# Retention heads scored in pairs, and three column sums moved from the index heads into the retention steps

## The chip, the cores and the metric

The kernel runs on one core of a Trainium2 chip. The metric is the device time of one execution in microseconds (us), lower is better. The core has a matrix engine (TensorE, PE in the profile; its weight loads are PEld), a vector engine (VectorE, DVE), an activation engine (ScalarE, ACT), GpSimd (POOL) and SyncE (SP), which issues most of the weight loads. Each engine works through its own instructions in the order written and waits on semaphores for the others. Matrix results land in PSUM banks of 128 x 512 floats.

## The reference, cut to what matters

Two transformer blocks on 256 tokens of width 1024, in float32. The second block has a modulation vector `mod = silu(c) @ w_ada + b_ada`, cut into six rows of 1024 (`sh1, sc1, g1, sh2, sc2, g2`), and three branches over one projection of the tokens. The part of concern:

```
mod = silu(c) @ w_ada + b_ada                     # sh1, sc1, g1, sh2, sc2, g2
# index scores (8 heads of 64): relu(q k^T), weighted, summed; top 64 keys of a query are kept
# retention (8 heads, keys of 64, values of 128):
scores = einsum('bnihd,bnjhd->bhnij', qc, kc) * intra_decay
o      = scores @ v + (carried state)             # here: one decayed 256 x 256 lower block matrix a head
y_ret  = (silu(g) * group_norm(o) * gain) @ w_ret_out
# sparse attention (8 heads of 64) over the kept keys
h  = h + g1 * ((ga*y_ret + gb*y_dsa) @ w_o)
u2 = rmsnorm(h)*(1 + sc2) + sh2 ;  h = h + g2 * experts(u2)
```

## The kernel before, in words

Every dense product is done in three passes of rounded float32 (high by high, high by low, low by high). Its weights pass as units of 128 x 1024: SP loads a unit, ACT writes its rounded high part (`split`, line 1158), DVE subtracts to get the low part (line 1911), PE multiplies it with the tokens (12 matrix instructions, lines 2924 to 2926, `three`). Between the small steps of the heads each engine's program has `fill(n)`, which puts in the next n units, so that PE has dense work while a head's softmax or decay is done by the others. The order on every engine is written out by hand.

Small products and transposes go into two "turn" banks that are used in turn. `plan_turns` lists their uses in order; `turn_bank` makes PE wait until the use two before has been copied out. Head scores go into the two banks of `sco`.

The modulation rows are accumulated over the weights of `w_ada`, leaving 128 partial rows in `mod`. They have to be added over the partitions and spread to all of them: PE multiplies 512 columns with a matrix of ones (`ada_sums`, line 3207) and ACT copies the bank back to `mod` (`ada_out`, `turned_copy`, line 1301). Of the twelve column blocks, nine are done earlier; the last three (9, 10, 11: the second halves of what scales and gates the expert part) are done in the stage looked at here.

The stages around the change, with their rows of the trace:

- Index heads (574 to 594.6 us). PE scores two heads at once from the upper and the lower half of the partitions (64 rows each) into the two score banks, then does `fill(IDX_FILL[g])`, then one `ada_sums`. ACT rectifies (line 1654), DVE adds to `mix` (lines 2458, 2460). After heads 1, 3 and 5 ACT has the copy of one column block. In the same stretch ACT and DVE prepare the retention gates (lines 1647, 2443, 2446).
- Retention (594.6 to 629.2 us), steps i = 0 to 8. PE: scores of head i into score bank i % 2 (lines 3546, 3547), one unit of dense work, then head i-1 is weighed (`weigh`, lines 3183 to 3185) from `probs_t`. PE scores head i once `decayed` says that head i-2 has been read. DVE, step i: decayed scores `probs_t = sco * decay` (line 2513), two of the sixteen rounds of the top-64 search (lines 2478, 2479), the low part of one unit, mean and variance of head i-1 (`ret_stats`, lines 2503, 2507), an evacuation of a dense block where one ends (line 1948), the gated product of head i-3 (`ret_out`, line 2494). POOL turns the variance into a scale (lines 984 to 1101). ACT, step i: the decay matrix of head i (`decay`, line 1681), the high part of one unit, in steps 0, 4 and 8 the tanh of a gate block (line 1247), then the scaled output of head i-2 (`ret_scale`, line 1668), which waits for POOL. `ret_scale` also frees the turn bank of that head.
- Start of the sparse attention (629.2 us on): PE scores sparse heads 0 and 1 (line 3561), does two units, transposes the gated retention rows (`turn_kept`, line 3143), ACT and DVE split them (lines 1283, 2045), and PE starts the product with `w_ret_out` (line 3027).

The column blocks are needed by DVE much later: line 2592 (`1 + sc2`), line 2878 and line 2900 (`g2`).

Of the kernel before, what the change touches and what calls it, by code (L numbers as in the profile page):

```python
# [11 lines left out]
ACT = mybir.ActivationFunctionType  # L12
AX = mybir.AxisListType

P = 128
D = 1024
S = 256
NT = S // P
DK = D // P
CHUNK = 64  # L20
HEADS = 8
W = 512
# [27 lines left out]
SC_W = P + S  # L50
# [20 lines left out]
RET_FILL = [1] * 9  # L71
# [91 lines left out]
def plan_turns():  # L163

    order = [(f"x1.{g}", "dve") for g in range(4)]
    order += [("bv", "act")]
    order += [(f"cl.{g}", "dve") for g in range(3)]
    order += [(f"qk{h}", "act") for h in range(2)]
    for h in range(HEADS + 2):
        if h + 2 < HEADS:
            order.append((f"qk{h + 2}", "act"))
        if 1 <= h <= HEADS:
            order.append((f"dap{h - 1}", "act"))
        if h == HEADS + 1:  # L180
            order.append(("oa.1", "dve"))
        if 2 <= h:
            order.append((f"dao{h - 2}", "dve"))
        if h == HEADS:
            order.append(("oa.0", "dve"))
    order += [("oa.2", "dve"), ("oa.3", "dve")]
    order += [("kr", "act")]
    for h in range(HEADS + 2):
        if 1 <= h <= HEADS:
            order.append((f"mp{h - 1}", "act"))  # L190
        if 2 <= h:
            order.append((f"mo{h - 2}", "dve"))
    order += [(f"mg.{g}", "dve") for g in range(4)]
    order += [(f"x2.{g}", "dve") for g in range(4)]
    order += [(f"ffn{e}", "dve") for e in range(N_FFN)]
    order += [("ad4", "act"), ("ad5", "act")]
    order += [(f"u.{g}", "dve") for g in range(4)]
    order += [("rt0", "act"), ("rt1", "act"), ("lt", "act"), ("rt2", "act"), ("lat", "act"), ("rt3", "act")]
    order += [("dt4", "act")]
    order += [(f"ad{n}", "act") for n in range(9, 12)]  # L200
    order += [(f"rto{h}", "act") for h in range(HEADS)]
    order += [("re.0", "dve"), ("re.1", "dve"), ("dsp0", "act"), ("re.2", "dve"), ("re.3", "dve")]
    for h in range(2, HEADS + 2):
        if h <= HEADS:
            order.append((f"dsp{h - 1}", "act"))
        if 2 <= h:
            order.append((f"dso{h - 2}", "dve"))
    order += [(f"mh.{g}", "dve") for g in range(4)]
    order += [(f"v.{g}", "dve") for g in range(4)]
    order += [("moe0", "dve"), ("moe0b", "dve")]  # L210
    order += [(f"moe{e}", "dve") for e in range(1, N_EXP)]
    order += [(f"moe{N_EXP - 1}b", "dve")]
    turns, count, names = {}, {"act": 0, "dve": 0}, []
    for number, (name, engine) in enumerate(order):
        count[engine] += 1
        turns[name] = (number, engine, count[engine])
        names.append(name)
    return turns, names
# [3 lines left out]
TURNS, TURN_NAMES = plan_turns()  # L222
# [127 lines left out]
def two_blocks(nc, ins, consts, one_hot_d, small_d, lambda_d, router_d, rel_rows, out):  # L350
    ctx = ExitStack()
    with ctx:
# [14 lines left out]
        def sem(name):  # L367
            return ctx.enter_context(nc.semaphore(name))
# [214 lines left out]
        ada_done = sem("ada_products_accumulated")  # L583
        shift_summed = sem("shift_and_scale_summed")
        shift_out = sem("shift_and_scale_copied")
        early_summed = sem("early_rows_summed")
        early_out = sem("early_rows_copied")
        gated_half = sem("retention_gates_begun")
# [544 lines left out]
        def _(act):  # L1133
# [259 lines left out]
            def ada_out(n0, n1):  # L1393

                for n in range(n0, n1):
                    turned_copy(f"ad{n}", [(mod[:, n * W:(n + 1) * W], bank_of(f"ad{n}"), 1.0)])
# [253 lines left out]
            for i in range(HEADS):  # L1650
                act.wait_ge(idx_scored, i + 1)
                if i >= 2:
                    act.wait_ge(idx_acc, i - 1)
                act.activation(probs[:, i % 2, 0, :], sco[:, i % 2, 0:SC_W], ACT.Relu).then_inc(relud, 1)
                if i % 2:
                    fill(IDX_FILL[i // 2])
                if i in (1, 3):
                    gate_rows(i // 2)
                if i in (1, 3, 5):
                    ada_out(9 + i // 2, 10 + i // 2)  # L1660

            def ret_scale(n):

# [10 lines left out]
            for i in range(HEADS + 2):  # L1674
                if i < HEADS:
                    if i < 2:
                        act.wait_ge(idx_acc, HEADS)
                    else:
                        act.wait_ge(decayed, i - 1)
                    g = float(np.log(np.float32(1.0 - 2.0 ** (-5.0 - i))))  # L1680
                    act.activation(probs[:, i % 2, 0, :], cst[:, C_DIST:C_DIST + SC_W], ACT.Exp, scale=g)\
                        .then_inc(decay, 1)
                if i <= HEADS:
                    fill(RET_FILL[i])
                if i >= 2:
                    ret_scale(i - 2)
            for i in range(HEADS + 2):
# [204 lines left out]
        def _(dve):  # L1892
# [695 lines left out]
            dve.nop().then_inc(evac["dve"], 1)  # L2588
            split_to(u_next + 4)
            dve.wait_ge(rows_in[0], 32)  # L2590
            dve.wait_ge(freed["act"], TURNS["ad9"][2])
            step.mark(dve.scalar_tensor_tensor(out=mod[:, 4 * D:5 * D], in0=mod[:, 4 * D:5 * D], scalar=1.0,
                                               in1=rows[:, 0, :], op0=ALU.add, op1=ALU.mult))
            rows_lo("mh", 1, 0.5)
# [267 lines left out]
            for p in range(1, N_EXP - 1):  # L2862
                u = gate_up_unit(p + 1) + AHEAD
                expert_lo(p)
                late = p + 2 < N_EXP and dense(p + 1) and not dense(p)
                for kt in (1, 3, 5):
                    if late and kt == 5:
                        split_around(u + 1 + kt // 2, lambda: expert_hidden(p + 1))
                    else:
                        split_to(u + 1 + kt // 2)  # L2870
                    side(p, kt)
                    if kt == 3 and closes_group(p):
                        slot_sums_lo(p)
                if p in (1, 2):
                    t = p - 1
                    dve.wait_ge(y_first_out, 2 * NT)
                    dve.wait_ge(freed["act"], TURNS["ad11"][2])
                    step(dve.tensor_tensor(y_first[t], y_first[t], mod[:, 5 * D:6 * D], ALU.mult))
                    step(dve.tensor_tensor(x[:, t, :], x[:, t, :], y_first[t], ALU.add))
                split_to(u + 4)  # L2880
                if p + 2 < N_EXP and not late:
                    expert_hidden(p + 1)
                side(p, "gate_up")
                split_to(u + 6)
                side(p, "down")
# [6 lines left out]
                                         op0=ALU.mult, op1=ALU.mult).then_inc(hid_ready, 1)  # L2892
                first_turn_lo(t)

            dve.wait_ge(freed["act"], TURNS["ad11"][2])
            halves = (slice(0, W), slice(W, D))
            for t in range(NT):
                for n, c in enumerate(halves):
# [19 lines left out]
        def _(pe):  # L2918
# [602 lines left out]
            for g in range(HEADS // 2):  # L3521
                if g:
                    pe.wait_ge(relud, 2 * g)
                halves = [slice(64 * a, 64 * a + 64) for a in range(2)]
                for a, r in enumerate(halves):
                    pe.matmul(sco[:, a, 0:P], idq_t[r, g, 0:P], idk_t[r, 0:P], start=True, stop=True)
                for a, r in enumerate(halves):
                    pe.matmul(sco[:, a, P:SC_W], idq_t[r, g, P:S], idk_t[r, 0:S], start=True, stop=True)\
                      .then_inc(idx_scored, 1)
                fill(IDX_FILL[g])  # L3530
                if g < 3:
                    ada_sums(9 + g, 10 + g)

            for i in range(HEADS + 1):
                if i == 0:
                    fill(RET_FILL[0])
                if i < HEADS:
                    pe.wait_ge(freed["act"], TURNS[f"rt{i // 2}"][2])
                    if i < 2:
                        pe.wait_ge(relud, HEADS)  # L3540
                    else:
                        pe.wait_ge(decayed, i - 1)
                    r = slice(64 * (i % 2), 64 * (i % 2) + 64)
                    q, k = rt_t[r, i // 2, 0:S], rt_t[r, i // 2, S:2 * S]
                    b = sco[:, i % 2, :]
                    pe.matmul(b[:, 0:S], k[:, 0:P], q[:, 0:S], start=True, stop=True)
                    pe.matmul(b[:, S:SC_W], k[:, P:S], q[:, P:S], start=True, stop=True).then_inc(ret_scored, 1)
                if i >= 1:
                    fill(RET_FILL[i])
                    h = i - 1  # L3550
                    pe.wait_ge(decayed, i)
                    weigh(f"rto{h}", probs_t[:, h % 2, :], [zz[:, t, RV + h * P:RV + (h + 1) * P] for t in range(NT)],
                          P)

            def sparse_scores(i):

# [20 lines left out]
            def kept_rest(part):  # L3577
# [3 lines left out]
                    unit_rest("ro0", part, t)  # L3581
                unit_at[0] += 1

            sparse_scores(0)
            fill(DSA_FILL[0])
            turn_kept(0)
# [414 lines left out]
```

## Time and profile before

| | |
|---|---|
| median of 3 runs | 909.11 us (909.02 to 909.26) |
| profiled execution, device time | 908.61 us |
| its span in the profile | 906.9 us |
| PE busy | 891.8 us (98%) |
| PE weight loads busy | 733.7 us (81%) |
| DVE busy | 680.7 us (75%) |
| ACT busy | 548.2 us (60%) |
| POOL busy | 209.7 us (23%) |

The span leaves out what lies before the first and behind the last instruction. A busy time is the union of the instructions' own times; matrix instructions are pipelined, one of 128 x 512 lasts 0.39 us and the next starts 0.23 us after it.

### The profile page before, as it was taken

To read this page: it belongs to the slowest core of one execution; us is meant where nothing else is said; L and a number is where in the kernel's file an instruction comes from. 1 tells how busy PE (TensorE), PEld (TensorE's weight loads), DVE (VectorE), ACT (ScalarE), POOL (GpSimd) and SP (SyncE) were. 2 spreads that over 40 slices of the span, in tenths; PEclk is the share of its full clock that TensorE was granted. 3 is DMA by queue.
4 is the path that set the end of the run, shared out by engine and by line. 5 is a ranking of instruction groups with operands and counts; after the bars stand their busy time and mean duration, and the time that the engine had idled before them with its cause. 6 is when DMAs were issued, how large, how long until landed. Compare 5 with 4: busy or idle time off the path is not lost.

```text
span 906.9 us, 12878 instructions
## 1 busy us (share of the span) xinstructions
PE 891.8 (98%) x4423; PEld 733.7 (81%) x4423; DVE 680.7 (75%) x961; ACT 548.2 (60%) x885; POOL 209.7 (23%) x218
## 2 busy tenths in 40 slices
PE   8999999999999999999999999999999999999996
PEld 6788877888887888888867889778788888888885
DVE  5867688765767578778786544699899897968984
ACT  6746776788557444443485445754775585656763
POOL 4696037545312011111005500014300000000001
PEclk9999999999999999999999999999999999999999
DMA  8656756666865989999646657634374098979941
GB/s 284 186 174 205 222 161 194 222 189 231 273 192 162 323 296 300 323 305 310 209 135 199 194 151 242 205 99 162 117 245 157 2 343 302 315 246 336 368 174 47
DMA packets 124007, 199.59 MB, mean 220 GB/s; under 512 B 9601, under 2 KB 73793, under 8 KB 123697
## 3 DMA queue, kind: packets, MB, share of 16 engines
q1 hardware_dynamic: 118048, 177.17, 59.9%
q0 software_dynamic: 5904, 21.71, 7.4%
q8 instruction: 31, 0.51, 0.2%
q14 instruction: 24, 0.20, 0.1%
HBM read 197.79 MB, written 2.62 MB: 221 GB/s over the span
## 4 chain that ended last, share of the span: by engine, by line
PE 83%; DVE 11%; issue 2%; ACT 1%; POOL 1%; DMA 1%; SPq 0%; ACTq 0%; DVEq 0%; POOLq 0%
PE lin L2924 21%; PE lin L2926 20%; PE lin L2925 20%; DVE w_lo L1911 3%; PE turn L3143 2%; PE sco L2926 2%; PE sco L2924 2%; PE sco L2925 2%; PE lin L3036 1%; PE lin L3037 1%; PE lin L3027 1%; PE sco L3264 1%; DMA raw<-in_w_in_dram 1%; PE lin L3705 1%; PE lin L3714 1%
## 5 line engine op out<-in xcount | busy, mean ns | idle before, releaser
L1911 DVE TENSOR_TENSOR w_lo<-raw,w_hi 128x1024 fp32r<-128x1024 f32 x220 | 288.4, 1323 | 105.2 <-ACT w_hi L1158 102.4
L1158 ACT ACTIVATE w_hi<-raw 128x1024 fp32r<-128x1024 f32 x220 | 229.0, 1059 | 106.6 <-PE lin L2926 84.8
L2924 PE MATMUL lin<-w_hi,a_hi 128*128 128x512 f32 (+2 forms) x600 | 237.2, 395 | 0.7 <-DVE w_lo L1911 0.5
L2926 PE MATMUL lin<-w_hi,a_lo 128*128 128x512 f32 (+2 forms) x600 | 230.7, 384 | 0.0
L2925 PE MATMUL lin<-w_lo,a_hi 128*128 128x512 f32 (+2 forms) x584 | 224.0, 384 | 0.0
L2924 PEld LDWEIGHTS lin<-w_hi,a_hi 128*128 128x128 f32 x600 | 112.8, 188 | 27.3 <-issue 4.4
L2926 PEld LDWEIGHTS lin<-w_hi,a_lo 128*128 128x128 f32 x600 | 112.8, 188 | 23.1
L2925 PEld LDWEIGHTS lin<-w_lo,a_hi 128*128 128x128 f32 x584 | 110.0, 188 | 20.0
L1122 POOL TENSOR_TENSOR arena<-x,rows 128x256 f32<-128x256 f32 x3 | 2.2, 736 | 195.3 <-DVE x L2902 195.2
L1064 POOL DMA_DIRECT2D arena<-in_w_ada_dram x32 | 16.9, 528 | 121.8 <-DVE mod L2014 121.3
L1038 POOL TENSOR_TENSOR mod<-mod,rows 128x1024 f32<-128x1024 f32 x16 | 38.1, 2383 | 24.9 <-ACT rows L1451 24.5
L1906 DVE TENSOR_TENSOR arena_r<-arena,w_lo 128x2048 fp32r<-128x2048 f32 x17 | 39.0, 2291 | 5.7 <-ACT w_lo L1152 5.5
L2014 DVE SCALAR_TENSOR_TENSOR mod<-arena,c_col,mod 128x1024 f32 x32 | 40.9, 1278 | 0.0
L991 POOL TENSOR_SCALAR stat<-stat 128x2 f32<-128x2 f32 (+1 forms) x22 | 7.9, 360 | 129.2 <-ACT idk_t L1313 128.4
L1152 ACT ACTIVATE w_lo<-arena 128x2048 fp32r<-128x2048 f32 x17 | 32.6, 1919 | 3.2 <-PE lin L2926 3.2
L2924 PE MATMUL lin<-w_hi,b_hi 128*128 128x512 f32 x82 | 32.6, 397 | 0.0
L2926 PE MATMUL lin<-w_hi,b_lo 128*128 128x512 f32 x82 | 32.0, 390 | 0.0
L2924 PE MATMUL lin<-w_hi,arena_r 128*128 128x512 f32 x76 | 30.5, 401 | 0.0
L3036 PE MATMUL lin<-w_lo,a_hi 128*128 128x512 f32 x72 | 28.7, 399 | 1.3 <-DVE w_lo L1911 1.3
L1331 ACT ACTIVATE probs<-sco,stat 128x128 f32<-128x128 f32 (+1 forms) x48 | 19.6, 418 | 16.7 <-DVE stat L2083 16.7
L2926 PE MATMUL lin<-w_hi,arena_r 128*128 128x512 f32 x76 | 29.7, 391 | 0.0
L1523 ACT ACTIVATE arena<-lin,stat 128x256 f32<-128x256 f32 x20 | 8.4, 471 | 33.0 <-PE lin L2926 33.0
(572 smaller groups left out, 1886.5 us busy)
## 6 DMA issues: line engine op xcount, KB each, us to landing
raw<-in_w_in_dram SPq DMA_DIRECT2D x76, 512.0 KB, 3.9
arena<-in_w_ada_dram POOLq DMA_DIRECT2D x32, 512.0 KB, 5.9
raw<-in_w_ffn_gate_dram SPq DMA_DIRECT2D x22, 512.0 KB, 5.0
raw<-in_w_ffn_up_dram SPq DMA_DIRECT2D x22, 512.0 KB, 6.1
raw<-in_w_ffn_down_dram SPq DMA_DIRECT2D x22, 512.0 KB, 4.0
rows<-in_w_ada_dram SPq DMA_DIRECT2D x16, 512.0 KB, 4.4
raw<-in_w_o_dram SPq DMA_DIRECT2D x16, 512.0 KB, 4.6
raw<-in_w_gate_dram SPq DMA_DIRECT2D x16, 512.0 KB, 4.8
```

Of the source, the lines that this page charges most:

```text
L1038: pool.tensor_tensor(acc, acc, early_slots[n % 3], ALU.add).then_inc(ada_done, 1)
L1152: act.activation(hi_tiles(u, n), raw_tiles(u, n), ACT.Copy).then_inc(hi_ready, n)
L1158: act.activation(w_hi[:, s, :], raw[:, s, :], ACT.Copy).then_inc(hi_ready, 1)
L1331: i = act.activation(dst, src, ACT.Exp, bias=st("nmax", k, 1), accum_out=st("rsum", k, 1))
L1906: dve.tensor_tensor(lo_tiles(u, n), raw_tiles(u, n), hi_tiles(u, n).bitcast(F32), ALU.subtract)\
L1911: dve.tensor_tensor(w_lo[:, s, :], raw[:, s, :], w_hi[:, s, :].bitcast(F32), ALU.subtract)\
L2014: dve.scalar_tensor_tensor(out=acc, in0=ada_slots[k % n_s], scalar=c_col[:, k:k + 1], in1=acc, op0=ALU.mult, op1=ALU.add).then_inc(ada_don ...
L2924: pe.matmul(dst, l_hi, r_hi, start=start, stop=False)
L2925: pe.matmul(dst, l_hi, r_lo, start=False, stop=False)
L2926: return pe.matmul(dst, l_lo, r_hi, start=False, stop=stop)
L3036: pe.matmul(lin[:, bank + t, :], hi[:, kt, c], wl[:, k, :], start=False, stop=False)
L3143: i = pe.transpose(b[0:n, at:at + m], src, ident[0:m, 0:m])
```

## The change

PE scores retention heads two at a time, as the index heads are: both banks of `sco` are filled by one call, for heads 0 and 1 before step 1, and for heads 2 and 3, 4 and 5, 6 and 7 at the end of steps 2, 4 and 6. The three column sums leave the index heads. They are now issued at the end of retention steps 3, 5 and 7, into score bank 0, which stands empty there. ACT copies them to `mod` in its steps 4, 6 and 8, ahead of `ret_scale`. PE waits for the first copy before it scores heads 4 and 5, for the second before heads 6 and 7, for the third before the first sparse heads. The three uses of the turn banks (`ad9`, `ad10`, `ad11`) are gone from the plan, so each later use has the other of the two banks.

```
 plan_turns:
-    order += [(f"ad{n}", "act") for n in range(9, 12)]
 ACT, index heads:
-                if i in (1, 3, 5):
-                    ada_out(9 + i // 2, 10 + i // 2)
 ACT, retention step i:
                 if i <= HEADS:
                     fill(RET_FILL[i])
+                if i in (4, 6, 8):
+                    n = 9 + (i - 4) // 2
+                    act.wait_ge(late_summed, n - 8)
+                    act.activation(mod[:, n * W:(n + 1) * W], sco[:, 0, :], ACT.Copy).then_inc(late_out, 1)
                 if i >= 2:
                     ret_scale(i - 2)
 DVE (three places, lines 2591, 2877, 2895):
-            dve.wait_ge(freed["act"], TURNS["ad9"][2])       # and "ad11"
+            dve.wait_ge(late_out, 1)                         # and 3
 PE, index heads:
                 fill(IDX_FILL[g])
-                if g < 3:
-                    ada_sums(9 + g, 10 + g)
 PE, retention:
-            for i in range(HEADS + 1):
-                ...
+            def retention_scores(i):
+                pe.wait_ge(freed["act"], TURNS[f"rt{i // 2}"][2])
+                halves = [slice(64 * a, 64 * a + 64) for a in range(2)]
+                q, k = rt_t[:, i // 2, 0:S], rt_t[:, i // 2, S:2 * S]
+                for a, r in enumerate(halves):
+                    pe.matmul(sco[:, a, 0:S], k[r, 0:P], q[r, 0:S], start=True, stop=True)
+                for a, r in enumerate(halves):
+                    pe.matmul(sco[:, a, S:SC_W], k[r, P:S], q[r, P:S], start=True, stop=True).then_inc(ret_scored, 1)
+
+            fill(RET_FILL[0])
+            pe.wait_ge(relud, HEADS)
+            retention_scores(0)
+            for i in range(1, HEADS + 1):
+                fill(RET_FILL[i])
+                h = i - 1
+                pe.wait_ge(decayed, i)
+                weigh(f"rto{h}", probs_t[:, h % 2, :], [zz[:, t, RV + h * P:RV + (h + 1) * P] for t in range(NT)], P)
+                if i % 2 == 0 and i < HEADS:
+                    if i >= 4:
+                        pe.wait_ge(late_out, i // 2 - 1)
+                    retention_scores(i)
+                elif i % 2 and i >= 3:
+                    n = 9 + (i - 3) // 2
+                    pe.matmul(sco[:, 0, :], ones[:, :].broadcast_to([P, P]), mod[:, n * W:(n + 1) * W],
+                              start=True, stop=True).then_inc(late_summed, 1)
 PE, sparse attention:
+            pe.wait_ge(late_out, 3)
             sparse_scores(0)
```

## Rows read from the trace of the kernel before

**Rows 1.** The page: busy times of all engines, and the chain that ended last.
```profile
PE 891.8 (98%) x4423; PEld 733.7 (81%) x4423; DVE 680.7 (75%) x961; ACT 548.2 (60%) x885; POOL 209.7 (23%) x218
...
PE 83%; DVE 11%; issue 2%; ACT 1%; POOL 1%; DMA 1%; SPq 0%; ACTq 0%; DVEq 0%; POOLq 0%
```

**Rows 2.** Windows: us, length, busy of PE, PEld, DVE, ACT, POOL, clock, DMA.
```profile
0.00:10.00 10.00, 6.45 (x35) 5.66 (x35) 1.95 (x6) 4.36 (x8) 2.83 (x8) 1.00 0.77 246
...
594.64:629.23 34.59, 34.59 (x178) 28.65 (x177) 32.94 (x101) 19.69 (x32) 8.17 (x24) 1.00 0.44 138
...
640.32:682.25 41.93, 41.72 (x216) 33.09 (x214) 40.60 (x75) 30.60 (x63) 5.67 (x10) 1.00 0.60 196
682.25:906.90 224.65, 217.10 (x1022) 179.07 (x1022) 182.29 (x226) 136.30 (x157) 4.49 (x7) 0.99 0.66 229
```

**Rows 3.** Timeline of PE, index heads: start, us, line, operation, idle before it.
```profile
585.15 1.02 PE L3207 MATMUL turn<-mod,ones 128*128 128x512 f32 x2
586.10 0.49 PE L3526 MATMUL sco<-idk_t,mod 64*128 64x128 f32 x4
```

**Rows 4.** Timeline of PE, retention and start of the sparse heads.
```profile
594.64 0.71 PE L3546 MATMUL sco<-arena 64*128 64x256 f32 x4
...
595.50 0.50 PE L2924 MATMUL lin<-w_hi,a_hi 128*128 128x512 f32 x1
...
604.43 0.50 PE L2924 MATMUL lin<-w_hi,a_hi 128*128 128x512 f32 x1
...
607.27 0.39 PE L3183 MATMUL turn<-arena,probs_t 128*128 128x128 f32 x2
...
608.03 0.70 PE L3546 MATMUL sco<-arena 64*128 64x256 f32 x2
...
608.88 0.50 PE L2924 MATMUL lin<-w_hi,a_hi 128*128 128x512 f32 x1
...
629.23 0.49 PE L3561 MATMUL sco<-idk_t,mod 64*128 64x128 f32 x4
...
635.64 0.60 PE L3143 MATMUL turn<-cst,arena 128*128 128x128 f32 x4
636.84 0.63 PE L3143 MATMUL turn<-cst,arena 128*128 128x128 f32 x4 [0.59 <-ACT arena L1668]
```

**Rows 5.** Timeline of DVE, index heads to the first sparse head.
```profile
587.58 1.64 DVE L2460 SCALAR_TENSOR_TENSOR mix<-probs,arena,mix 128x128 f32<-128x128 f32 x4 [0.39 <-ACT probs L1654]
...
611.71 0.55 DVE L2513 SCALAR_TENSOR_TENSOR probs_t<-sco,probs 128x384 f32<-128x384 f32 x1
...
616.28 0.55 DVE L2513 SCALAR_TENSOR_TENSOR probs_t<-sco,probs 128x384 f32<-128x384 f32 x1
...
620.85 0.55 DVE L2513 SCALAR_TENSOR_TENSOR probs_t<-sco,probs 128x384 f32<-128x384 f32 x1
...
632.38 0.53 DVE L2535 SCALAR_TENSOR_TENSOR probs<-sco,probs 128x384 f32<-128x384 f32 x1
```

**Rows 6.** Timeline of ACT, index heads to the first sparse head.
```profile
586.20 0.60 ACT L1301 ACTIVATE mod<-turn 128x512 f32<-128x512 f32 x1 [1.50 <-PE turn L3207]
587.05 0.87 ACT L1654 ACTIVATE probs<-sco 128x384 f32<-128x384 f32 x2 [0.25 <-PE sco L3528]
...
608.00 0.81 ACT L1668 ACTIVATE arena<-turn,stat 128x128 f32<-128x128 f32 x2 [1.26 <-POOL stat L1101]
...
610.31 1.04 ACT L1247 ACTIVATE arena<-arena 128x1024 f32<-128x1024 f32 x1
...
617.82 0.80 ACT L1668 ACTIVATE arena<-turn,stat 128x128 f32<-128x128 f32 x2 [2.17 <-POOL stat L1101]
...
628.82 1.04 ACT L1247 ACTIVATE arena<-arena 128x1024 f32<-128x1024 f32 x1
...
635.89 0.81 ACT L1668 ACTIVATE arena<-turn,stat 128x128 f32<-128x128 f32 x2 [1.86 <-POOL stat L1101]
636.81 0.60 ACT L1283 ACTIVATE a_hi<-turn 128x512 fp32r<-128x512 f32 x1
```

More of the change, by code:

```diff
@@ L585, in two_blocks @@
         shift_out = sem("shift_and_scale_copied")
+        late_summed = sem("last_rows_summed")
+        late_out = sem("last_rows_copied")
         early_summed = sem("early_rows_summed")
@@ L2876, in _ @@
                     dve.wait_ge(y_first_out, 2 * NT)
-                    dve.wait_ge(freed["act"], TURNS["ad11"][2])
+                    dve.wait_ge(late_out, 3)
                     step(dve.tensor_tensor(y_first[t], y_first[t], mod[:, 5 * D:6 * D], ALU.mult))
@@ L2893, in _ @@
                 first_turn_lo(t)
-            dve.wait_ge(freed["act"], TURNS["ad11"][2])
+            dve.wait_ge(late_out, 3)
             halves = (slice(0, W), slice(W, D))
@@ L3530, in _ @@
                 fill(IDX_FILL[g])
-                if g < 3:
-                    ada_sums(9 + g, 10 + g)
-            for i in range(HEADS + 1):
[L3535 to L3553, printed above, removed]
+            def retention_scores(i):
[6 more added lines that the diff above has]
+                    pe.matmul(sco[:, a, S:SC_W], k[r, P:S], q[r, P:S], start=True, stop=True).then_inc(ret_scored, 1)
```

## The prediction

> **What bounds the kernel now.** I read the busy times and the chain first. PE is busy 98% of the span and carries 83% of the chain; DVE carries 11% of it [rows 1]. Taken for the whole kernel, PE time saved is time saved. The table by stage says otherwise for the retention stage: in its 34.59 us PE has no gap at all, but DVE is busy 32.94 us of them (95%), and the next 42 us look the same, 40.60 of 41.93 [rows 2]. What DVE lacks to 100% there are turnarounds, not waits: asked for waits between 595 and 629 us, the trace names none, for DVE or for PE. So I read the two timelines side by side. PE's step takes 4.45 us: a unit of dense work from 604.43 to 607.27 (2.84), the weighing of a head to 608.03 (0.76), the scores of one head to 608.88 (0.85) [rows 4]. DVE's step takes 4.57 us: the decayed product of head 4 starts at 611.71, of head 5 at 616.28, of head 6 at 620.85 [rows 5]. The scores of head 4 are there at 608.9, and DVE comes for them at 611.71. DVE sets the pace of this stage, with PE 2.8 us ahead at that place; from 682 us on PE is the bound (217 of 225 us busy, and 11.90 us of those are the last output steps) [rows 2], and it takes over whatever lateness it is handed.
>
> The Trainium skill, "Perfetto Trace Analysis", section "Identifying the Most-Contended Engine", has it that matmul busy time is a poor measure for TensorE, that the share of weight loads is the better one, and that occupancy is fair for VectorE. In this stage weight loads fill 28.65 of 34.59 us, 83%, against DVE's 95% [rows 2]. By the matmul rows the change would save its PE time in full; by the rule it saves none of it. The first is my rival D below.
>
> **The change, part by part.** I keep the profiled execution (908.61 us, 0.5 below the median of 909.11) as the base and add the same difference to the median.
>
> *Pairs.* Before, heads 0 and 1 already stand together: 594.64 to 595.50, 0.86 us for both [rows 4]. The six others cost 0.85 each. After: four pairs at 0.86. PE saves 6 x 0.85 - 3 x 0.86 = 2.5 us of work, all of it in a stage that DVE paces. Here it is worth nothing.
>
> *Sums and copies leave the index heads.* Each sum takes PE 0.95 us (585.15 to 586.10) [rows 3], each copy ACT 0.60 [rows 6]. PE reaches the end of that stage 2.85 us earlier. DVE gains only where it waited for scores: 0.39 us at 587.58, behind the rectified scores of heads 4 and 5, which had waited for PE behind two sums [rows 5, 6]. Ahead of it DVE has its own evacuation, so no more than 0.39 comes. All of DVE runs 0.39 earlier from there: -0.39.
>
> *Sums into retention steps.* 0.95 us of PE each in steps 3, 5, 7. A matrix product of this shape into `sco` has no row; into a turn bank it is 0.95. I take that; even at twice the price it would be covered, since PE then waits anyway, as follows.
>
> *The new waits.* This is the part that I expect to cost. PE may not score heads 4 and 5 before ACT has emptied bank 0, and ACT does that in its step 4, behind `ret_scale(1)`, a decay matrix, a split and a tanh. `ret_scale(1)` hangs on DVE's statistics by way of POOL and runs at 608.00; the tanh starts 2.31 us later, at 610.31, and takes 1.04 [rows 6]. With DVE 0.39 earlier, the tanh ends at 611.35 - 0.39 = 610.96, the copy (0.60) at 611.56. An ACT result reaches waiting PE 0.14 us after its end (635.89 + 0.81 to 636.84 [rows 4, 6]): the pair starts at 611.70. A pair is read 0.95 after its start (586.10 to 587.05 [rows 3, 6]): 612.65. DVE would come at 611.71 - 0.39 = 611.32 [rows 5]. It waits 1.33 us, and behind this product stand its top-64 rounds, the low part of a unit and the statistics of head 3. DVE is now 612.65 - 611.71 = 0.94 us later than before. PE was ready for the pair earlier: it ended weighing head 3 at 608.03 + 4.45 = 612.48 before, and now has 2.85 + 0.84 + 0.85 less and 0.95 more in front, so 608.9 at the earliest and about 610 with what it waits for DVE and ACT on the way; it stands 1.5 to 2.8 us.
>
> Heads 6 and 7: the same again. `ret_scale(3)` follows DVE and comes at 617.82 + 0.94 = 618.76. There is no tanh in step 6, so the copy starts 2.31 later, 621.07, and ends 621.67; pair at 621.81, read at 622.76. DVE before: 620.85; would come at 621.79, so it waits 0.97 more. It is now 622.76 - 620.85 = 1.91 us later than before.
>
> The sparse heads: the third copy stands behind the tanh of step 8. 628.82 + 1.04 + 1.91 = 631.77, copy until 632.37, PE at 632.51 in place of 629.23: 3.28 late [rows 4, 6]. DVE comes for these scores at 632.38 + 1.91 = 634.29 and finds them (632.51 + 0.95 = 633.46) [rows 5], so no third wait of DVE. But PE's two units and the first transposes of retention rows now start at 635.64 + 3.28 = 638.92 and end 0.60 later [rows 4]. Before, ACT had the last `ret_scale` until 636.70 and split these rows at 636.81, which PE had ready in time; now ACT is free at 638.6 and waits for PE until 639.52 + 0.03 = 639.55, 2.74 us later than 636.81 [rows 4, 6]. The low part on DVE, the first product with `w_ret_out` and the exponentials of the sparse heads all follow this.
>
> *What takes it back.* Between 640 and 682 neither PE (0.21 us idle) nor DVE has room, and beyond 682 PE is the bound [rows 2]. I find nothing that absorbs it. The sum: -0.39, +1.33, +0.97, and another 0.83 by PE's lateness at the sparse heads = +2.74.
>
> *What is free.* The three waits of DVE on `late_out` come at 689 us and later; copies end at 632. The turn banks swap, but every use still waits for the one two before. The first retention heads no longer wait for banks of the sums, but for older ones. No DMA is moved: SP and POOL keep their order, and raw slots come free by DVE's low parts.
>
> The Trainium skill, "TensorEngine Tiling (Array Packing)", section "Key Properties", says that changing the tiling mode drains TensorE. The 64-row scores between 128-row products change mode seven times before and four times after. If a change cost more than the 0.85 of a head already holds, the pairs would save more PE time; as DVE paces the stage, the sum stays.
>
> **Forecast.** 909.11 + 2.7 = 911.8 us, 0.30% slower. For itself this case reaches from 910.9 to 912.8: each of the two handovers of ACT, PE and DVE may be off by 0.3, and the third by as much.
>
> **The rivals.**
>
> B. Only part of it arrives. The margins are small: if ACT empties the bank 1 us earlier in steps 4 and 6 (a tanh is 1.04), DVE waits 0.3 in the first and not in the second, and the third wait delays PE by about 1.4 instead of 3.3, inside what DVE and POOL leave open before 636.8. Or PE makes up 0.8 later. +0.5 to +1.8; middle 910.2. For it: ACT has idle time in each step (1.26 and 2.17 us ahead of `ret_scale` [rows 6]). Against: that idle lies before `ret_scale`, and the copy after it.
>
> C. The waits fall where nobody stands. Then DVE keeps its pace and only the 0.39 is left: 908.7, no change. It needs the first copy to end by 611.32 - 0.95 - 0.14 = 610.23, and my sum has 611.56.
>
> D. PE's time counts. If DVE's dense row of instructions is itself released by PE's units, the 2.5 us of saved work come off the end: 906.6. For it: PE without a gap in 34.59 us [rows 2]. Against: the scores lie ready 2.8 us before DVE takes them, and DVE shows no wait for PE. This is the rival on the other side. It decides if DVE's products of heads 4 and 6 start earlier than before, below 611.7 and 620.9.
>
> E. PE stands still three times for 1 to 3 us, and its granted clock falls to 1.2 GHz behind that. Each dense unit at half speed would take 2.84 more; one such unit on the path gives 914.6, two give 917. Against: the first 10 us have PE idle for 3.55 us and the granted clock is at its upper level, 1.00, in them [rows 2].
>
> **How the numbers follow.** Chances: forecast 0.53, B 0.19, C 0.10, D 0.13, E 0.05. A measurement of this kernel tells 0.2% (1.8 us) from no change, so same is 907.3 to 910.9: B and C, 0.29. Faster is D, 0.13. Slower is the forecast and E, 0.58. For the range I leave out most of D, and what of E lies above one slow unit: 908.2 to 913.4. The forecast's own range is above.
>
> **What would show it.** In the profile after: PE waits for ACT (copy from `sco` to `mod`) before the pairs of heads 4/5 and 6/7 and before the sparse heads, 1.5 to 2.8, about 1 to 2, and about 2 us long; DVE waits for PE before the products of heads 4 and 6, 1.3 and 1.0; the product of head 4 starts at 612.6 in place of 611.7, that of head 6 at 622.8 in place of 620.9; the index stage gives DVE 0.4; the first transposes of retention rows start 3.3 later; from 640 us to the end one constant shift of 2.7. It would be wrong if DVE shows no wait for PE in the retention stage (then C or D), if the shift shrinks between 640 and 682 (B), or if a slice behind a wait has a granted clock below 1.00 (E).

## The result: 911.29 us against 909.02 us

| | before | after |
|---|---|---|
| median of 13 executions | 909.02 us (908.53 to 909.26) | 911.29 us (910.34 to 913.12) |
| profiled execution, device time | 908.61 us | 912.80 us |
| its span in the profile | 906.9 us | 911.1 us |

The ratio is 1.0029 (95% interval 1.0022 to 1.0037), +2.27 us. The forecast was 911.8, +2.7. The profiled execution is one of the dearer ones, for a reason that its rows show.

Line numbers of the kernel after are 3 higher on DVE and for PE's dense units, weighing and transposes, and 1 lower or higher on ACT; PE's retention scores are L3542 and L3544, the moved sum L3560, the sparse scores L3569. The page and the waits, to be held against [rows 1] (columns of the waits: engine, line that waited, who released it, us in total, times, longest):

```profile
PE 891.8 (98%) x4423; PEld 733.7 (81%) x4423; DVE 681.0 (75%) x961; ACT 547.9 (60%) x885; POOL 209.7 (23%) x218
...
PE 88%; DVE 6%; ACT 2%; issue 2%; DMA 1%; POOL 1%; SPq 0%; ACTq 0%; DVEq 0%; POOLq 0%
```

```profile
DVE probs_t L2516 <- PE sco L3544: 1.8, 2, 1.0
...
PE sco L3542 <- ACT mod L1687: 2.5, 2, 1.4
PE sco L3569 <- ACT mod L1687: 1.7, 1, 1.7
PE turn L3186 <- ACT arena L1667: 0.8, 1, 0.8
```

Busy times are nearly those of before: on the whole-kernel shares alone the change would seem to do nothing. The waits tell it. L1687 is ACT's copy of a sum out of score bank 0. PE stands for it at the pairs of heads 4/5 and 6/7 (L3542) and at the sparse heads (L3569), and DVE in turn stands for the scores of heads 4 and 6 (L2516). None of this was there before. The wait of the last line, 0.75 us at the weighing of head 2 (L3186, for the turn bank that `ret_scale` of head 0 frees), is new too; it stays in the copies-first kernel below, at no cost.

PE's timeline after (start, length, line, operation, idle before it and its releaser), against [rows 4]:

```profile
605.89 1.02 PE L3560 MATMUL sco<-mod,ones 128*128 128x512 f32 x2
...
611.74 0.70 PE L3542 MATMUL sco<-arena 64*128 64x256 f32 x4 [1.40 <-ACT mod L1687]
...
621.73 0.70 PE L3542 MATMUL sco<-arena 64*128 64x256 f32 x4 [1.07 <-ACT mod L1687]
...
632.24 0.49 PE L3569 MATMUL sco<-idk_t,mod 64*128 64x128 f32 x4 [1.66 <-ACT mod L1687]
...
633.56 0.63 PE L2928 MATMUL lin<-w_lo,a_hi 128*128 128x512 f32 x1
633.98 0.63 PE L2929 MATMUL lin<-w_hi,a_lo 128*128 128x512 f32 x1
...
636.54 0.47 PE L2929 MATMUL lin<-w_hi,a_lo 128*128 128x512 f32 x1
636.85 0.40 PE L2927 MATMUL lin<-w_hi,a_hi 128*128 128x512 f32 x1
...
640.27 0.93 PE L3146 MATMUL turn<-cst,arena 128*128 128x128 f32 x7
```

ACT's, against [rows 6]: the tanh (L1248) ahead of the first and third copy, and the split (L1284) of the first transposed rows of retention.

```profile
610.16 1.04 ACT L1248 ACTIVATE arena<-arena 128x1024 f32<-128x1024 f32 x1
611.11 0.57 ACT L1687 ACTIVATE mod<-sco 128x512 f32<-128x512 f32 x1
...
621.10 0.58 ACT L1687 ACTIVATE mod<-sco 128x512 f32<-128x512 f32 x1
...
630.66 1.04 ACT L1248 ACTIVATE arena<-arena 128x1024 f32<-128x1024 f32 x1
631.61 0.58 ACT L1687 ACTIVATE mod<-sco 128x512 f32<-128x512 f32 x1
...
640.91 0.60 ACT L1284 ACTIVATE a_hi<-turn 128x512 fp32r<-128x512 f32 x1 [2.38 <-PE turn L3146]
```

DVE's, against [rows 5]. The first row lies far ahead of all that the change touches; it is needed because two executions don't reach that point at the same time.

```profile
542.29 1.23 DVE L1914 TENSOR_TENSOR w_lo<-raw,w_hi 128x1024 fp32r<-128x1024 f32 x1 [2.55 <-ACT w_hi L1159]
...
587.48 1.64 DVE L2463 SCALAR_TENSOR_TENSOR mix<-probs,arena,mix 128x128 f32<-128x128 f32 x4
...
607.27 0.55 DVE L2516 SCALAR_TENSOR_TENSOR probs_t<-sco,probs 128x384 f32<-128x384 f32 x1
...
612.69 0.56 DVE L2516 SCALAR_TENSOR_TENSOR probs_t<-sco,probs 128x384 f32<-128x384 f32 x1 [1.04 <-PE sco L3544]
...
622.68 0.56 DVE L2516 SCALAR_TENSOR_TENSOR probs_t<-sco,probs 128x384 f32<-128x384 f32 x1 [0.76 <-PE sco L3544]
...
641.54 0.69 DVE L2048 TENSOR_TENSOR a_lo<-turn,a_hi 128x512 fp32r<-128x512 f32 x1 [2.46 <-ACT a_hi L1284]
```

Three rows of DVE before that were not needed for the prediction, and are for this comparison:

```profile
541.92 1.22 DVE L1911 TENSOR_TENSOR w_lo<-raw,w_hi 128x1024 fp32r<-128x1024 f32 x1 [2.56 <-ACT w_hi L1158]
...
607.42 0.55 DVE L2513 SCALAR_TENSOR_TENSOR probs_t<-sco,probs 128x384 f32<-128x384 f32 x1
...
637.44 0.69 DVE L2045 TENSOR_TENSOR a_lo<-turn,a_hi 128x512 fp32r<-128x512 f32 x1 [0.21 <-ACT a_hi L1283]
```

The profiled execution after is 0.37 us late at 542 already. That is not the change's: its first edit acts behind that row, among the index heads. Counted from that row, the change stands as follows.

| DVE at | before | after | change, so far |
|---|---|---|---|
| product of head 3 | 65.50 | 64.98 | -0.52 |
| product of head 4 | 69.79 | 70.40 | +0.61 |
| product of head 6 | 78.93 | 80.39 | +1.46 |
| low part of the first retention rows | 95.52 | 99.25 | +3.73 |

The last step, 2.27 us, is larger than a wait. The windows say why (columns: stretch, length, busy of PE, PEld, DVE, ACT, POOL, granted clock, DMA share, GB/s):

```profile
629.00:632.00 3.00, 1.58 (x10) 1.12 (x8) 2.86 (x9) 2.83 (x5) 0.74 (x1) 1.00 0.11 41
634.00:636.00 2.00, 2.00 (x6) 1.62 (x5) 1.93 (x7) 0.81 (x2) 1.81 (x4) 0.50 0.59 217
637.00:640.00 3.00, 3.00 (x15) 2.48 (x14) 0.66 (x2) 0.81 (x2) 2.92 (x6) 1.00 0.51 175
...
686.50:911.10 224.60, 216.98 (x1022) 179.14 (x1022) 182.16 (x226) 136.37 (x157) 4.49 (x7) 0.99 0.66 228
```

Behind the third idle the granted clock is 0.50, 1.2 GHz, for the products from 633.6 to 636.5: each lasts 0.63 us and the next follows 0.42 to 0.43 behind it, where the same instructions elsewhere take 0.39 and follow 0.23 apart. From the sparse scores to the first transposes PE takes 640.27 - 632.24 = 8.03 us; before it took 635.64 - 629.23 = 6.41 [rows 4]. So the low clock costs 1.62 here, and what is left of the change is 3.73 - 1.62 = 2.11. From the low clock on nothing is given back: from the transposes at 682.25 to the end the kernel before takes 224.65 us [rows 2], and from the same transposes, which start at 686.38 after, it is 911.10 - 686.38 = 224.72 (the last window above begins 0.12 behind them).

Only one execution was traced. Of the 13, four have a mean granted clock of 0.996 and take 912.1 to 913.1 us; the nine others have 0.997 or 0.998 and take 910.3 to 911.7, their median 911.01, +1.99. The traced one is of the four. That the other three had the same slow stretch is likely by their times, and not shown.

### The profile page after: what moved, and what is told of

The parts are those of the page before. It is cut to its first block, busy times and chain, and to the rows that moved or that the text cites. A ratio compares the mean times of both kernels' runs of the same rounds, so it can differ in the third digit from the quotient of the medians.

```text
span 911.1 us, 12870 instructions
## 1 busy us (share of the span) xinstructions
PE 891.8 (98%) x4423; PEld 733.7 (81%) x4423; DVE 681.0 (75%) x961; ACT 547.9 (60%) x885; POOL 209.7 (23%) x218
## 4 chain that ended last, share of the span: by engine, by line
PE 88%; DVE 6%; ACT 2%; issue 2%; DMA 1%; POOL 1%; SPq 0%; ACTq 0%; DVEq 0%; POOLq 0%
PE lin L2927 21%; PE lin L2929 21%; PE lin L2928 21%; PE turn L3146 3%; PE sco L2929 2%; PE sco L2927 2%; PE sco L2928 2%; PE lin L3039 1%; PE lin L3040 1%; PE lin L3030 1%; DVE w_lo L1914 1%; PE turn L3194 1%; DMA raw<-in_w_in_dram 1%; PE sco L3267 1%; PE lin L3714 1%
```

## Experiments

The theory, W: the time is lost because ACT's copy comes late in its step, PE cannot score the next pair until it has, and DVE, which paces the stage, waits for PE; the low clock is an extra behind PE's idles in some executions. Rivals: P, the pairs themselves cost; D of the prediction, PE's time counts for the stage; E of the prediction, taken further: the clock is the main part of the loss.

A scale for all of them is the way from the DVE row at 542 to the first transposes of the stage that follows (PE's 8 transposes of `arena`), which takes out what an execution has lost or gained ahead of 542. The rows before and after:

```profile
682.25 1.09 PE L3143 MATMUL turn<-cst,arena 128*128 128x128 f32 x8 [0.15 <-DVE arena L1977]
```

```profile
686.38 1.09 PE L3146 MATMUL turn<-cst,arena 128*128 128x128 f32 x8 [0.15 <-DVE arena L1980]
```

Before: 682.25 - 541.92 = 140.33. After: 686.38 - 542.29 = 144.09, 3.76 more. Each kernel has one trace; its median is that of all its executions.

| kernel | way from 542, against 140.33 | median, against that of before beside it |
|---|---|---|
| changed | +3.76 (2.14 without the low clock) | +2.27 |
| copies first | -0.52 | -0.57 |
| pairs only | +1.01 | +0.59 |
| sums only | +7.35 | +6.98 |
| PE kept busy | +2.19 | +2.08 |
| third copy first | +1.44 | +1.11 |
| more work on DVE | +2.34 | +2.44 |
| gated products on GpSimd | -2.00 | -1.49 |

One trace and the median agree to about half a microsecond, except for the changed kernel, where they do so only without the low clock of the traced execution.

**Copies first.** The changed kernel with ACT's copy at the head of its step, before the decay matrix, the split and the tanh. All else stays.

```
 ACT, retention step i:
+                if i in (4, 6, 8):
+                    n = 9 + (i - 4) // 2
+                    act.wait_ge(late_summed, n - 8)
+                    act.activation(mod[:, n * W:(n + 1) * W], sco[:, 0, :], ACT.Copy).then_inc(late_out, 1)
                 if i < HEADS:
                 ...
                     fill(RET_FILL[i])
-                if i in (4, 6, 8):
-                    ...
```

> The changed kernel with ACT's three copies moved to the head of their steps, ahead of the decay matrix, the split and the tanh; nothing else. Theory W (what costs is the place of the copy in ACT's order: PE waits for it, and DVE waits for the scores behind it): the first copy ends near 609.3 instead of 611.7, PE's three waits of 1.4, 1.1 and 1.7 us shrink below 0.5 in all, DVE's waits for scores of heads 4 and 6 go, the time is 908.4 to 909.2. Rival P (the pairs or the sums in the retention steps cost by themselves, wherever ACT copies): 910.5 or more. Rival D (PE's saved work counts once nothing waits): 906.5 to 907.5.

Measured: 908.54 us (11 runs), ratio 0.9993 (0.9984 to 1.0002). ACT, DVE and the two waits that PE still has between 590 and 660 us:

```profile
608.94 0.60 ACT L1677 ACTIVATE mod<-sco 128x512 f32<-128x512 f32 x1
...
610.79 1.05 ACT L1248 ACTIVATE arena<-arena 128x1024 f32<-128x1024 f32 x1
```

```profile
611.71 0.55 DVE L2516 SCALAR_TENSOR_TENSOR probs_t<-sco,probs 128x384 f32<-128x384 f32 x1
...
620.84 0.55 DVE L2516 SCALAR_TENSOR_TENSOR probs_t<-sco,probs 128x384 f32<-128x384 f32 x1
```

```profile
PE turn L3146 <- ACT arena L1667: 1.1, 1, 1.1
PE turn L3186 <- ACT arena L1667: 0.8, 1, 0.8
```

The copy now lies at 608.94, ahead of the tanh in place of behind it, and all waits for copies and for scores are gone, with the whole loss. The place of three copies of 0.6 us in ACT's order is the cause: W. It also decides D. This kernel scores in pairs, so PE has 2.5 us less to do in the stage. Its row of 542 stands at 542.45, 0.53 later than before. Counted from there DVE is 0.53 early at heads 3 and 4 and 0.54 at head 6, and the way ends 0.52 short: that is the gain of the index heads, no more. From head 3 (607.42) to head 6 DVE takes 13.42 us, before 13.43. That the products of heads 4 and 6 stand on the clock at the times of before to 0.01 [rows 5] is a coincidence of the two executions. The time that PE saves is idle time of PE. What the Trainium skill states in "Perfetto Trace Analysis", section "Identifying the Most-Contended Engine", that occupancy is a fair measure for VectorE and matmul time a poor one for TensorE, picked the right engine of the two here (95% against PE's 100% of matmul time and 83% of loads [rows 2]).

**Pairs only.** The kernel before with retention heads scored in pairs; the sums stay among the index heads.

```
+            for i in range(1, HEADS + 1):
+                fill(RET_FILL[i])
+                ...
+                if i % 2 == 0 and i < HEADS:
+                    retention_scores(i)
```

> The kernel before with the retention heads scored in pairs; the three sums and copies stay with the index heads. Theory W: PE has 2.5 us less work in a stage that DVE paces, the time stays within 0.3 of the kernel before, 908.7 to 909.3. Rival D (PE paces): 906.5. Rival P (pairs hurt, because head scores come later or lock both banks): 909.8 or more.

Measured: 909.70 us (11 runs), ratio 1.0008 (0.9999 to 1.0017). That is between what W (up to 909.3) and P (from 909.8) gave, and the times leave open whether this is slower. The trace has a wait that neither the kernel before nor the changed one has (PE, then DVE):

```profile
603.06 0.70 PE L3541 MATMUL sco<-arena 64*128 64x256 f32 x4
```

```profile
604.01 0.56 DVE L2513 SCALAR_TENSOR_TENSOR probs_t<-sco,probs 128x384 f32<-128x384 f32 x1 [0.87 <-PE sco L3543]
```

Scored singly, head 2 has its scores ahead of its step's dense unit, at 599.14 in the trace of before; as half of a pair it comes behind that unit and the weighing of head 1, at 603.06. DVE waits 0.87 for it, and 1.01 is the way lost. So P holds here, in one trace: without the sums moved, pairs cost rather than give. In the changed kernel this wait does not appear: with the sums gone from the index heads PE scores heads 2 and 3 at 600.54, 2.5 us earlier.

**Sums only.** The changed kernel with retention heads scored singly at the head of each step, as before.

```
+            for i in range(HEADS + 1):
+                if i < HEADS:
+                    if i in (4, 6):
+                        pe.wait_ge(late_out, i // 2 - 1)
+                    ...                               # scores of head i
+                if i >= 1:
+                    fill(RET_FILL[i])
+                    ...                               # weigh head i - 1, then the sum in steps 3, 5, 7
```

> The changed kernel with heads scored one at a time as before; sums, score bank 0 and ACT's copies are where the change has them, and head 4 and head 6 wait for the copy. Theory W: the waits are those of the changed kernel, since ACT copies at the same place: DVE waits about 1.0 and 0.8 us for heads 4 and 6, time 910.6 to 911.6. Rival P (it is the pairs): 909.0. PE waits less than in the changed kernel, as it has 2.5 us more to do.

Measured: 916.09 us (5 runs), ratio 1.0084 (1.0070 to 1.0097): far above what either theory gave. PE, and the granted clock behind its wait:

```profile
605.07 1.02 PE L3559 MATMUL sco<-mod,ones 128*128 128x512 f32 x2
610.88 1.22 PE L3549 MATMUL sco<-arena 64*128 64x256 f32 x2 [4.79 <-ACT mod L1687]
```

```profile
610.80:614.80 4.00, 3.92 (x10) 3.02 (x11) 2.13 (x7) 1.36 (x4) 1.17 (x4) 0.50 0.91 302
```

The expectation overlooked the order of PE. With single scores the wait stands right behind the sum, and the dense unit of the step stands behind the wait, so PE idles 4.79 us and not 1.4, and goes on at 1.2 GHz. In the pair order a unit and a weighing lie between sum and wait (606.35 to 610.34 in the changed kernel). Against before, counted from 542, DVE is 1.33 late at head 4, 4.04 at head 6 and 7.35 at the low part of the first retention rows; how much of that is the low clock was not parted. It is the order that comes with the pairs which makes the moved sums bearable; neither half of the change can be judged without the other. Whether single scores in another order would do as well was not tried.

**PE kept busy.** The changed kernel with small products in PE ahead of its three waits, five, five and seven calls.

```
+                        keep_clock(5)
                         pe.wait_ge(late_out, i // 2 - 1)
                         ...
+            keep_clock(7)
             pe.wait_ge(late_out, 3)
```

> The changed kernel with small products written over the free score bank 1 ahead of PE's three waits (about 1.2, 1.2 and 1.7 us of work, about the length of the waits). Theory K (two costs: the waits, about 2.1 us, and in some executions a stretch at 1.2 GHz behind them, about 1.6 us more): the granted clock stays at 1.00 in 600 to 645 us, median 910.7 to 911.2, and the runs lie within 0.8 of each other instead of 2.8. If PE's idle time has nothing to do with the clock: again a slice near 0.5 behind the third wait, and a spread of over 2. If the added products were on the path: above 911.8.

Measured: 911.19 us (11 runs, 910.40 to 911.54), ratio 1.0023 (1.0014 to 1.0032). PE ahead of the sparse heads and behind, and DVE's first wait:

```profile
630.44 1.73 PE L3217 MATMUL sco<-cst 128*128 128x128 f32 x14
632.27 0.49 PE L3570 MATMUL sco<-idk_t,mod 64*128 64x128 f32 x4
...
633.47 0.40 PE L2928 MATMUL lin<-w_lo,a_hi 128*128 128x512 f32 x1
```

```profile
612.71 0.56 DVE L2516 SCALAR_TENSOR_TENSOR probs_t<-sco,probs 128x384 f32<-128x384 f32 x1 [1.05 <-PE sco L3544]
```

PE's idle is filled, the products behind it stay at 0.40, and DVE's waits are as they were. The highest of 11 times is 911.54, against 913.12 of 13 for the changed kernel, and none of the 11 has a mean granted clock below 0.997; the medians differ by 0.10. The spread, 1.14, is more than the 0.8 expected. This parts the loss in two: the waits cost about 2.1, the low clock about 1.6 more in some executions. That none of 11 fell by chance, where 4 of 13 seem to have fallen, is unlikely and not excluded. As the main part the clock is refuted; as a tail it is there.

**Third copy first.** The changed kernel with the third copy alone at the head of ACT's step 8; the first two stay behind the tanh and the split.

> The changed kernel with only the third copy (ACT's step 8) at the head of its step; the first two stay behind the split and the tanh. Theory W prices the three waits apart: DVE's two waits for scores together 1.9 us, and the third, which holds up only PE, another 0.8. So DVE keeps its waits of about 1.0 and 0.8 us, PE's third wait shrinks below 0.4, ACT splits the first retention rows at once behind its last scaled head, the time is 910.2 to 910.8, and since PE no longer stands 1.7 us there, no execution falls to 1.2 GHz behind it. Rival: the third wait is hidden anyway, time as the changed kernel, 911.3. Other rival: it is the whole price, 909.

Measured: 910.00 us (11 runs), ratio 1.0016 (1.0007 to 1.0025). DVE, at head 4 and at the low part of the first retention rows:

```profile
611.75 0.56 DVE L2520 SCALAR_TENSOR_TENSOR probs_t<-sco,probs 128x384 f32<-128x384 f32 x1 [1.04 <-PE sco L3548]
...
638.34 0.69 DVE L2052 TENSOR_TENSOR a_lo<-turn,a_hi 128x512 fp32r<-128x512 f32 x1 [0.21 <-ACT a_hi L1284]
```

PE, at the first sparse heads:

```profile
629.56 0.49 PE L3573 MATMUL sco<-idk_t,mod 64*128 64x128 f32 x4
```

The first two waits are there in full, the third is gone, and 1.44 of the way is left: the first two terms and the gain, 1.46 after head 6 in the changed kernel. The third wait is worth 2.14 - 1.44 = 0.7 without the low clock; the expectation had 0.8, and its range, 910.2 to 910.8, lies just above the median. With two idles in place of three the granted clock is 1.00 from 600 to 645 us, and no execution is above 911.35.

**More work on DVE.** The kernel before with a `memset` of 128 x 1024 on DVE ahead of the products of heads 4 and 6: pure lateness of DVE, PE untouched.

> The kernel before with one more DVE instruction at the head of retention steps 4 and 6 (a memset of 128 x 1024 floats that nobody reads; no wait for PE in it). Theory W (DVE sets the pace here, and what it loses is lost at the end): each instruction delays the product behind it by its own duration, the end moves by the sum of both, about 1 to 2.2 us: 910.1 to 911.3. Rival D (PE paces, DVE has room): within 0.3 of the kernel before.

Measured: 911.33 us (9 runs), ratio 1.0027 (1.0018 to 1.0037).

```profile
612.14 0.91 DVE L2512 MEMSET tmp<- 128x1024 f32 x1 [0.16 <-issue]
613.09 0.56 DVE L2515 SCALAR_TENSOR_TENSOR probs_t<-sco,probs 128x384 f32<-128x384 f32 x1
```

Each holds DVE for 0.91 and the 0.16 ahead of it, 2.14 for both, and the product behind it starts 0.04 after its end, where it started 0.09 before the end of the instruction ahead of it in the kernel before. Counted from 542 (542.08 here) the product of head 4 is 1.22 late and that of head 6 2.41. The way grows by 2.34, the median by 2.44, a little more than the 2.2 expected. What DVE is late in this stage arrives at the end in full, which is the price that the prediction set on its waits.

**Gated products on GpSimd.** Copies first, and five of the eight gated products of retention (heads 0 to 4) move from DVE to GpSimd, which multiplies each behind the statistics of the next head.

```
 GpSimd, ahead of its heads:
+            pool.wait_ge(rows_used, 5)
 GpSimd, for head n:
+                if 1 <= n <= HEADS - 3:
+                    pool.wait_ge(ret_scaled, n)
+                    v = zz[:, :, RV + (n - 1) * P:RV + n * P]
+                    pool.tensor_tensor(v, v, zz[:, :, RG + (n - 1) * P:RG + n * P], ALU.mult).then_inc(ret_done, 1)
 DVE, retention step i:
-                if i >= 3:
-                    ret_out(i - 3)
 DVE, ahead of the last three gated products:
+            dve.wait_ge(ret_done, HEADS - 3)
```

> The kernel with all copies first in their steps, and in addition the gated products of retention heads 0 to 4 (128 x 256 each, 0.4 to 0.7 us on DVE) done by GpSimd, which is idle there. Theory W: DVE is what bounds the stage once nothing waits, so 2.3 us less on DVE let the top-64 search, the statistics and the last scaled head come earlier, and PE, now 2.5 us lighter, can follow: 906.6 to 907.6. If the saving on DVE is given back by slower DVE instructions beside GpSimd's, or by GpSimd's statistics coming later: 908.2 or more. Rival D: as the kernel with the copies first, 908.5.

Measured: 907.40 us (11 runs), ratio 0.9983 (0.9974 to 0.9992). GpSimd, then DVE at heads 4 and 6:

```profile
607.00 0.74 POOL L1108 TENSOR_TENSOR arena<-arena 128x256 f32<-128x256 f32 x1
```

```profile
610.52 0.56 DVE L2521 SCALAR_TENSOR_TENSOR probs_t<-sco,probs 128x384 f32<-128x384 f32 x1
...
619.28 0.56 DVE L2521 SCALAR_TENSOR_TENSOR probs_t<-sco,probs 128x384 f32<-128x384 f32 x1 [0.19 <-PE sco L3548]
```

It beats both kernels, the one before by 1.49 us. Against copies first the way is 1.48 shorter, 0.30 for each product taken off DVE. The time that the pairs save on PE begins to count here: DVE waits for scores again, 0.19 for head 6, so PE and DVE are now close to even in this stage.

## Why the prediction came out as it did

**Which engine paces.** Right. In copies first DVE's steps from head 3 to head 6 take 13.42 us against 13.43 although PE has 2.5 us less to do, and DVE's lateness in more work on DVE passes to the end in full. Rival D needed 2.5 us off the end; with the waits gone the way is 0.52 shorter, all of it from the index heads.

**Pairs worth nothing.** Right for the changed kernel, but the step named no price for them alone. Pairs only shows one, 1.0 us of way: head 2 is scored a unit later. PE's earlier arrival covers it.

**Sums leaving the index heads, -0.39.** The idle ahead of 587.58 [rows 5] is gone in the row at 587.48; counted from 542 DVE is 0.52 earlier at head 3. A little more than forecast, and hidden in a plain comparison of two spans by the 0.37 that this execution had lost before.

**The new waits.** This is the step that carries the sum. PE's pairs were forecast for 611.70 and 621.81 and start at 611.74 and 621.73; DVE was forecast at 612.65 and 622.76 and comes at 612.69 and 622.68; the sparse scores for 632.51, measured 632.24. In terms of way the first wait costs 1.13 (forecast 1.33) and the second 0.85 (0.97). PE's own idles, 1.40, 1.07 and 1.66, are at or just below what was named (1.5 to 2.8, about 1 to 2, about 2). The copies, 0.57 and 0.58 in place of 0.60, and their start behind `ret_scale` (611.11 - 607.86 = 3.25, forecast 3.35; 621.10 - 618.80 = 2.30, forecast 2.31) nearly hold. That the times on the clock fit to 0.1 is in part luck: the whole execution stood 0.37 late, and the waits are each a little shorter.

**The third wait, +0.83.** Right in kind: PE's transposes come late, ACT's split waits for them (2.38 at 640.91), DVE's low part for it. Without the low clock it costs 3.73 - 1.46 - 1.62 = 0.65.

**Nothing takes it back.** Right: 224.65 us against 224.72 from those transposes to the end, and from the low part of the first retention rows to the first transposes of the next stage it is 44.81 us before (682.25 - 637.44) and 44.84 after (686.38 - 641.54), so rival B's later recovery is out, as its missing waits are by the rows above. C is out by the two waits of DVE.

**The sum.** -0.52 + 1.13 + 0.85 + 0.65 = 2.11, against -0.39 + 1.33 + 0.97 + 0.83 = 2.74. All four terms err to the same side, by 0.12 to 0.20. For the first wait the rows say why. Taken back by the 0.37, the first pair starts at 611.37, 0.33 before its forecast: DVE, and ACT behind it, had gained 0.13 more in the index heads; the copy starts 0.09 before the printed end of the tanh and is 0.03 shorter; and PE follows its end by 0.06 (611.68 to 611.74) where 0.14 was taken. The same small surpluses stand in the later terms. The median has +2.27, in which a little of the low clock is left; without the four executions it is +1.99.

**Rival E.** It was given 0.05 on the ground that 3.55 us of idle in the first 10 us leave the clock at its upper level [rows 2]. That was a poor witness: in the traced execution the clock fell behind idles of 1.40, 1.07 and 1.66 us, each shorter than the 2.88 with which the kernel before begins and behind which it is at 1.00. The prediction's own sign of E, a slice behind a wait with a granted clock below 1.00, is there in that execution. Its price was also off, 2.84 forecast for a unit at half speed and 1.62 measured, since the clock rose again within the two units. In the traced execution it makes 1.62 of 3.76, and going by the times it is in 4 of 13; it moves the median by little (911.29 of all 13, 911.01 of the other nine), which is why the forecast stands. How often it would come was no part of the sum, and that it came seldom is luck.

## What to carry to other kernels

When a result is parked in a buffer that another engine needs next, what it costs is set by where the emptying instruction stands in its own engine's order, not by its length: three copies of 0.6 us behind a tanh and a split cost 2.66 us of way more than at the head of their steps (2.14 against -0.52). Before counting a saving on the busiest engine, see whether its neighbour has any gap to give; here 2.5 us taken off PE bought nothing while DVE had no gap. Where a thing stands in the order can matter more than whether it is there: pairs alone cost, sums alone cost far more. Compare two traces from a row that lies ahead of the change, not from the start of the span.

## What the runs showed of the hardware that was not expected

TensorE's granted clock fell to 0.50, 1.2 GHz, for some 3 us behind the last of three idles of 1.40, 1.07 and 1.66 us, with dense work at 0.39 us a product in between, and came back while PE was at work. Behind the first two it was 1.00, and in third copy first, which has only those two, it stayed there. The Trainium skill, "TensorE: Matmul & The Clock Gate", section "HAM oscillation — how this bites in real kernels", tells of a kernel whose waits throw the engine back to the lower level again and again; here it happened once in the traced execution, and going by the times in about a third of them, with the same program. In sums only, one idle of 4.79 us had 0.50 behind it as well (610.80 to 614.80). With the idles filled by small products all of the 11 executions stayed between 910.40 and 911.54. That the idles bring the fall is what these runs suggest; each kernel has one trace, so it is not proven.

A 64-row pair of heads costs PE what a single head does: 612.59 - 611.74 = 0.85 for two, 0.85 for one [rows 4].

GpSimd takes 0.74 us for the gated product of 128 x 256 (607.00 in gated products on GpSimd). DVE takes 0.40, with 0.31 until its next instruction starts (611.40 in the trace of before).
